# Alternating the two column halves' PSUM banks at each matmul of the weight product

## The reference

```python
# first block
mod = silu(c) @ ada_w + ada_b                      # 2048 -> 3 * 2048, one row
h = rms_norm(x, norm_g) * (1 + scale) + shift
proj = h @ w_in                                    # attention and recurrence inputs
mix = concat([o_a, o_r]) @ w_out
x = x + gate * mix
# second block, two layers
m = pool_mixer(h, w_pool) or diff_attention(h, k, v, ...)   # k, v = rmsnorm(x) @ w_kv; q = h @ w_q; ... @ w_o
x = x + rmsnorm(m, norm_mix_post)
x = x + rmsnorm((silu(h @ w_gate) * (h @ w_up)) @ w_down, norm_ffn_post)
```

## Time and profile before

| | |
|---|---|
| median of 3 runs | 2760.87 us (2760.17 to 2760.97) |
| span of the profiled execution, first to last instruction | 2756.0 us |
| outside the span (median less span) | 4.9 us |
| PE busy | 2610.5 us (95%) |
| DVE, ACT busy | 1416.6 us (51%), 1117.2 us (41%) |
| mean granted TensorE clock | 0.973 |

### The profile page before, as it was taken

One profiled execution on the slowest core, in us unless ns is written; L12 is line 12 of the kernel. 1 busy time (PEld: TensorE's weight loads), 2 busy tenths in 40 slices (PEclk: granted clock), 3 DMA queues, 4 the chain that ended last, 5 costly groups with the idle time before them and its releaser, 6 DMA issues. The chain is left out here.

```text
span 2756.0 us, 31637 instructions
## 1 busy us (share of the span) xinstructions
PE 2610.5 (95%) x11812; PEld 2101.0 (76%) x11812; DVE 1416.6 (51%) x1286; ACT 1117.2 (41%) x1046; POOL 310.5 (11%) x271
## 2 busy tenths in 40 slices
PE   5799999997987999999999999998989999999997
PEld 1388888855876888888888778887778888888886
DVE  6764435457456444444444455576454444444444
ACT  4634323334344343343333344454443434333332
POOL 7100059901002000000000002200010000000000
PEclk8899999998989999999999999999999999999999
DMA  8845536553524554646546455543445655555463
GB/s 288 330 159 192 177 138 228 190 176 108 198 87 156 185 204 161 214 162 217 207 160 229 168 165 195 190 146 133 173 153 184 197 183 185 196 183 214 161 221 122
DMA packets 185620, 505.31 MB, mean 183 GB/s; under 512 B 17680, under 2 KB 17968, under 8 KB 184128
## 3 DMA queue, kind: packets, MB, share of 16 engines
q1 hardware_dynamic: 183472, 493.63, 51.5%
q0 software_dynamic: 1536, 8.37, 1.0%
q10 hardware_dynamic: 528, 2.16, 0.2%
HBM read 502.01 MB, written 2.10 MB: 183 GB/s over the span
## 5 line engine op out<-in xcount | busy, mean ns | idle before, releaser
L1281 DVE TENSOR_TENSOR lo<-raw,hi 128x2048 fp32r<-128x2048 f32 (+1 forms) x390 | 916.7, 2351 | 1022.8 <-ACT hi L932 1022.2
L932 ACT ACTIVATE hi<-raw 128x2048 fp32r<-128x2048 f32 (+1 forms) x390 | 744.9, 1910 | 1145.2 <-PE acc L502 1109.6
L500 PE MATMUL acc<-hi,h_hi 128*128 128x512 f32 (+1 forms) x2688 | 1057.4, 393 | 31.6 <-DVE h_lo L1351 11.2
L502 PE MATMUL acc<-hi,h_lo 128*128 128x512 f32 (+1 forms) x2688 | 1049.8, 391 | 0.0
L501 PE MATMUL acc<-lo,h_hi 128*128 128x512 f32 (+1 forms) x2688 | 1049.3, 390 | 0.0
L500 PEld LDWEIGHTS acc<-hi,h_hi 128*128 128x128 f32 x2688 | 510.3, 190 | 141.4 <-DVE lo L1281 19.7
L502 PEld LDWEIGHTS acc<-hi,h_lo 128*128 128x128 f32 x2688 | 509.8, 190 | 105.7
L501 PEld LDWEIGHTS acc<-lo,h_hi 128*128 128x128 f32 x2688 | 510.7, 190 | 102.4
L500 PE MATMUL acc<-hi,g_hi 128*128 128x512 f32 x704 | 274.0, 389 | 0.0
L502 PE MATMUL acc<-hi,g_lo 128*128 128x512 f32 x704 | 273.9, 389 | 0.0
L501 PE MATMUL acc<-lo,g_hi 128*128 128x512 f32 x704 | 273.9, 389 | 0.0
(11 more groups left out here) (282 smaller groups left out, 1378.1 us busy)
## 6 DMA issues: line engine op xcount, KB each, us to landing
raw<-in_w_ffn_gate SPq DMA_DIRECT2D x176, 512.0 KB, 3.8
raw<-in_w_ffn_up SPq DMA_DIRECT2D x176, 512.0 KB, 4.7
raw<-in_w_ffn_down SPq DMA_DIRECT2D x176, 512.0 KB, 4.1
raw<-in_w_in SPq DMA_DIRECT2D x144, 512.0 KB, 4.3
raw<-in_ada_w SPq DMA_DIRECT2D x96, 512.0 KB, 4.9
raw<-in_w_kv SPq DMA_DIRECT2D x64, 512.0 KB, 4.5
raw<-in_w_out SPq DMA_DIRECT2D x32, 512.0 KB, 4.1
raw<-in_w_q SPq DMA_DIRECT2D x32, 512.0 KB, 3.5
```

What stands on the lines that cost most here:

```text
L500: pe.matmul(o, l_hi, w_hi, start=first, stop=False)
L502: mm = pe.matmul(o, l_lo, w_hi, start=False, stop=last)
L932: act.activation(hi_slots[slot][:, 0:st.cols], raw[:, r, 0:st.cols], ACT.Copy).then_inc(hi_made, 1)
L1281: vec.tensor_tensor(lo_slots[slot][:, 0:st.cols], raw[:, r, 0:st.cols], hi_slots[slot][:, 0:st.cols], ALU.subtract).then_inc(slab_split, 1)
```

## The change

Inside one slab and one token tile, the loop over the two column halves moves inside the loops over k-tile and over the three terms. Both banks' `acc_free` are waited for ahead of the first matmul, and the signals that a bank is done are attached to the last two matmuls.

```diff
             for t in range(st.tiles):
-                for n in ([s] if st is st_pool else range(st.halves)):
-                    b = st.bank(t, n)
-                    if s == 0 or st is st_pool:
-                        pe.wait_ge(acc_free[b], g + (st.bank0[b] + 1))
-                    for kk in range(st.kt):
...
-                        pe.matmul(o, l_hi, w_hi, start=first, stop=False)
-                        pe.matmul(o, l_hi, w_lo, start=False, stop=False)
-                        mm = pe.matmul(o, l_lo, w_hi, start=False, stop=last)
+                ns = [s] if st is st_pool else list(range(st.halves))
...
+                if s == 0 or st is st_pool:
+                    for n in ns:
+                        pe.wait_ge(acc_free[st.bank(t, n)], g + (st.bank0[st.bank(t, n)] + 1))
+                for kk in range(st.kt):
...
+                    if st is st_ada:
+                        for o, w in zip(banks, w_hi):
+                            pe.matmul(o, st.lhs(k), w, start=first, stop=False)
+                        mms = [pe.matmul(o, st.lhs(k), w, start=False, stop=last) for o, w in zip(banks, w_lo)]
+                        continue
+                    l_hi, l_lo = st.lhs(k, t)
+                    for o, w in zip(banks, w_hi):
+                        pe.matmul(o, l_hi, w, start=first, stop=False)
+                    for o, w in zip(banks, w_lo):
+                        pe.matmul(o, l_hi, w, start=False, stop=False)
+                    mms = [pe.matmul(o, l_lo, w, start=False, stop=last) for o, w in zip(banks, w_hi)]
+                for n, mm in zip(ns, mms):
                     ends_slab = (t == st.tiles - 1) and (st is st_pool or n == st.halves - 1)
                     if ends_slab:
                         mm.then_inc(slab_used, 1)
                     elif last:
-                        mm.then_inc(acc_done[b], 1)
+                        mm.then_inc(acc_done[st.bank(t, n)], 1)
```

More of the change, by code:

```diff
@@ new lines, in product @@
+                ns = [s] if st is st_pool else list(range(st.halves))
+                banks = [acc[0:2, st.bank(t, n), :] if st is st_ada else acc[:, st.bank(t, n), 0:st.width] for n in ns]
+                if s == 0 or st is st_pool:
+                    for n in ns:
+                        pe.wait_ge(acc_free[st.bank(t, n)], g + (st.bank0[st.bank(t, n)] + 1))
+                for kk in range(st.kt):
+                    k = s * st.kt + kk
+                    first, last = k == 0, k == kts - 1
+                    if st is st_pool:
+                        k, first, last = (2 * g + s) * 4 + kk, kk == 0, kk == 3
+                    offs = [(kk if st is st_pool else kk * st.halves + n) * st.width for n in ns]
+                    w_hi = [hi_slots[slot][:, a:a + st.width] for a in offs]
+                    w_lo = [lo_slots[slot][:, a:a + st.width] for a in offs]
+                    if st is st_ada:
[9 more added lines that the diff above has]
+                    mms = [pe.matmul(o, l_lo, w, start=False, stop=last) for o, w in zip(banks, w_hi)]
```

## The result

The changed kernel takes 2774.12 us (median of 4 executions, 2770.01 to 2776.21) beside 2760.92 us for the kernel before in the same comparison (4 executions). The ratio is 1.0046, 95% interval 1.0034 to 1.0058. It is slower, as forecast, but by more: the mean of all nine executions is 2772.0 us, and that of before 2760.6, so 11.4 us where I forecast 7.2. That is inside the wide range (2762.5 to 2774) and above the band of the forecast (2764.5 to 2771.5). It also scatters more (2767.4 to 2776.2; 23 executions of before lie within 2758.4 to 2764.1). One more execution of before, 5087.27 us at a granted clock of 0.89, ran in a slower state and is left out. The question behind the prediction is what the other 4 us are.

A forecast was written before the change was run, and what follows sets the result against it. PE's stream of matmuls bounds the kernel, busy 2610.5 of 2756.0 us. Terms 1.48 + 1.35 + 0.53 + 0.2 + 1.13 + 1.50 + 0.31 + 0.69 = 7.2 us, added to 2760.87, gave 2768.1 us, range 2762.5 to 2774.

The forecast's parts named there:

- k, q and v: Four boundaries from k to v: PE stops for bank 1, 4 x 0.37 = 1.48 us; v's middle was taken as 0.2.
- pace term of 0: All matmuls: changing banks at every matmul leaves the step at 0.227 us, so the main effect is zero.
- both pace rivals: All matmuls: alternating banks saves time per matmul (2752 us at 2 ns, chance 0.06) or costs 1 ns (2776, chance 0.04).
- cover of 0.28 us: gu boundaries: bank 1 is free 0.28 us before its need, cost 0; rival of cover or clock lost, chance 0.08.
- 0.2 I had taken: Middle of v: PE is behind VectorE's attention work, so 0.2 us was taken between bounds 0 and 0.37.
- The middles: Middles of down0, o and down1: PE waits for bank 1, 0.45 us each, three times 1.35 us.
- ada's term: ada: PE waits 0.39 us for bank 1 and the end is 0.3 later, together 0.69 us, bounds 0 and 1.5.
- longer wait for mod_row: ada: the trace after would show PE's wait for mod_row grown by 3 x 0.39 us.
- tail terms: Stage ends where emptying is the path: out 1.13 us, down0, o and down1 together 1.50, v 0.31.
- all of it moves by 1.13 us: Out's end: VectorE's chain of four banks, started by bank 0's last matmul, moves 1.13 us later.
- the 0.50 at the end of down0: End of down0: ScalarE's chain of squaring banks ends 0.50 us later because bank 2 is done later.
- stops bring TensorE's clock down: Rival: ten new stops drop the clock to 1.2 GHz, 14 us, 2782; chance 0.08 together with lost cover.

The follow-up runs named there:

- e1: The changed kernel measured once more, no edit: 2770.76 us against 2760.61 for the kernel before, ratio 1.0036.
- e7: Kernel before, matmul order kept, with both the early waits for banks 1 and 3 and the late signals of banks 0 and 2: 2771.96 us, ratio 1.0045.
- e2: Kernel before with banks alternating in all slabs but the first and last of a group: 2760.47 us, ratio 0.9999.
- e4: Kernel before with banks alternating only in the last slab of a group, so late signals: 2767.29 us, ratio 1.0021.
- e6: Kernel before, matmul order and waits kept, only the done signals of banks 0 and 2 five slots later: 2769.14 us against 2759.92.
- e5: Kernel before, matmul order kept, only the waits for banks 1 and 3 moved early: 2765.38 us against 2759.92.
- e12: Changed kernel plus 27 matmuls with unread results at the end of out, keeping PE busy in its wait: 2769.5 us, ratio 1.0032.

## Why the prediction was right, and where it was too small

Measured between the starts of first and last matmuls of stages and groups, in profiled executions without fillers: the mean of the three with both kinds of event moved (after, e1, e7) less that of the two with none (before, e2). The first three rows hold much chance: single executions of all kernels lie 2.7, 2.4 and 3.4 us apart there.

| stretch | forecast, us | measured, us |
|---|---|---|
| start to the end of in1 (ada) | 0.69 | 1.7 |
| small and in2 | 0.53 | 0.9 |
| gate to the end of out, its middle | 0 | -1.0 |
| seam of out | 1.13 | 1.6 |
| gu, down0 with its middle | 0.45 | 0.50 |
| seam of k (end of down0) | 0.50 | 1.75 |
| k, q and v | 1.68 | 1.99 |
| end of v | 0.31 | 0.24 |
| o with its middle | 0.45 | 0.73 |
| end of o, first gu group | 0.50 | 1.06 |
| gu, down1 with its middle | 0.45 | 0.53 |
| end of down1 | 0.50 | 0.50 |
| sum | 7.2 | 10.5 |

- The sign and the mechanism hold. The pace term of 0, the step on which the sign rested, is shown by e2 and by e7, and with it both pace rivals fall. The step of 216 ns, which the Trainium skill has (TensorE: Matmul & The Clock Gate, Back-to-back issue gap), doesn't appear when banks alternate either: the rows stay at 227 ns.
- The gu boundaries cost 0 as forecast. The cover of 0.28 us held in all of them, through two waits in a row.
- Each stop and tail is where it was put. k, q and v are 0.3 larger, from v. The stop of 0.45 us at v's middle is won back in PE's next wait for VectorE's attention work; but the last of these waits, 42 us on (1869.93 before, 1882.31 after), grew from 1.53 to 1.97 us from start to start, 0.44 for the 0.2 I had taken between bounds of 0 and 0.37. The middles cost 0.50 to 0.73 for 0.45.
- ada's term is not settled. The longer wait for mod_row, its sign, did not come, and the group times hang on loads. The executions with both events moved reach in1's end 1.7 us later on average, more than the upper bound of 1.5, but single ones of all kernels lie between 356.2 and 358.9 us.
- The step that was mis-sized is the tail terms: "all of it moves by 1.13 us" at out, and the 0.50 at the end of down0. The chains did move by just that much. But I priced the move with the clock of the rows before. Both tails lead into a pause in which TensorE's clock falls, and moving the pause changes how long the clock is at half over the products behind it. At k that made 1.75 us of 0.50 in every execution with both events moved, and -1.4 where the signals alone were late (e4, e6). At out it made 3.3 of 1.13 on average over the six executions with the late signal, but the changed kernel's own (after, e1, e7) have 4.3, 0.3 and 0.3. Of the 3.3 us that the table is over 7.2, k's tail gives 1.25 and out's 0.5; by the average of six out's would be 2.2.
- A further 0.5 is in the first gu group behind o, all of it in e1: there the clock fell once more, behind a stop of 2 us inside that group (half clock from 2043.1 to 2046.5), and the stretch took 66.7 us in place of 65.2. e5 has the same fall.
- I had this as a rival ("stops bring TensorE's clock down") and gave it little, because I looked for it at the new stops of 0.2 to 0.6 us. There it did not come: the changed kernel's k, q and v stretch (the row below) has clock 1.00 throughout, stops included. That is also what speaks against the rule cited for it (the Trainium skill, TensorE: Matmul & The Clock Gate, A second HAM failure mode: psum-queue depth-cycling), as far as this kernel goes. The falls that cost time stand at pauses that were there already, of 2 to 11 us.

```profile
1651.71:1898.29 246.58, 243.16 (x1126) 200.23 (x1124) 144.24 (x191) 117.69 (x179) 30.88 (x48) 1.00 0.52 179
```

What stays open: whether out's seam loses its extra time as regularly as k's. Its six executions fall on 115.4, 118.5 to 119.4 and 122.6, and the mean clock over the seam falls with them, but what stands ahead of it (loads, GpSimd's work) varies, so I can't tell steps from chance. Open is also what makes whole executions scatter: e7's mean is 5.7 us above its profiled execution.

## What to carry to other kernels

Changing the PSUM bank at every matmul cost nothing here and gained nothing; what the order of a product decides is when each bank is finished and when it must be empty, and finishing banks one after another staggers both. Price a reordering by those two events at every group boundary and stage end, not by the pace. Where a tail leads into a long pause of TensorE, take the fall of its clock into the range: the products behind the pause can pay more than the tail moved, or less. What counts is the time at half clock over the products, not over the pause.

## What the hardware showed that I had not expected

- A delay of 0.5 us ahead of a pause made the stretch over that pause and the group behind it 1.4 us shorter (e4, e6), or, with the early waits as well, 1.75 us longer (after, e1, e7, e12), repeatably to 0.1 us.
- After a stop of 0.24 us the next step takes 0.34 us in place of 0.227 (e5): a stop costs about 0.1 us more than it lasts.
- Filling a pause keeps the clock at full (5.53 us in place of 9.72 for 48 matmuls of 128 columns), yet before k a filled pause saved nothing: the falls that lie over k's first products came all the same.
